# Dilated attention in one 16-stage kernel: scores in a token order by residue modulo four, run beside the last projection's matmuls

## The reference

```python
qkv = (h @ wqkv).reshape(b, s, 3, ng, A_HEADS, D_HEAD)
q, k = apply_rope(qkv[:, :, 0], cos, sin), apply_rope(qkv[:, :, 1], cos, sin)
...
wts = jax.nn.softmax(jnp.stack(lses, axis=0), axis=0)
o = jnp.sum(wts[..., None] * jnp.stack(outs, axis=0).astype(jnp.float32), axis=0).astype(h.dtype)
return o.reshape(b, s, A_HEADS * D_HEAD) @ wo
```

## Time and profile before

| | |
|---|---|
| median of 3 runs | 2399.34 us (2391.01 to 2400.08) |
| the profiled execution's own time | 2394.36 us |
| its span | 2392.5 us |
| PE busy in the span | 2285.8 us (96%) |
| DVE, ACT, POOL busy | 1485.6, 1158.6, 175.0 us |
| mean granted TensorE clock | 0.979 of 2.4 GHz |
| HBM read | 392.50 MB |

### The profile page before, as it was taken

One profiled execution on the slowest core, in us unless ns is written; L12 is line 12 of the kernel. 1 busy time (PEld: TensorE's weight loads), 2 busy tenths in 40 slices (PEclk: granted clock), 3 DMA queues, 4 the chain that ended last, 5 costly groups with the idle time before them and its releaser, 6 DMA issues.

```text
span 2392.5 us, 32798 instructions
## 1 busy us (share of the span) xinstructions
PE 2285.8 (96%) x12883; PEld 1846.9 (77%) x12883; DVE 1485.6 (62%) x2089; ACT 1158.6 (48%) x1672; POOL 175.0 (7%) x288
## 2 busy tenths in 40 slices
PE   8999899999998999799999999998999999979998
PEld 6888788887887668678877888857888788748886
DVE  6656657657665866576566657565655765647655
ACT  5445445446544453254455445444445544545444
POOL 1001001001001011310010000001000100041001
PEclk9999999999999999799999999999999999989999
DMA  7556546554656420165545555504555565506553
GB/s 246 189 182 217 184 156 210 191 190 145 213 175 214 163 99 4 37 196 179 193 167 187 192 188 195 178 18 135 178 193 184 169 193 184 194 4 207 177 184 106
DMA packets 289751, 395.68 MB, mean 165 GB/s; under 512 B 11672, under 2 KB 193248, under 8 KB 289600
## 3 DMA queue, kind: packets, MB, share of 16 engines
q1 hardware_dynamic: 284800, 377.33, 47.8%
q0 software_dynamic: 4656, 16.20, 2.0%
q10 hardware_dynamic: 144, 0.07, 0.0%
HBM read 392.50 MB, written 1.05 MB: 164 GB/s over the span
## 4 chain that ended last, share of the span: by engine, by line
PE 76%; DVE 5%; ACT 3%; issue 2%; POOL 1%; DMA 1%; DVEq 0%; POOLq 0%; ACTq 0%; SPq 0%
PE bank L490 22%; PE bank L492 22%; PE bank L491 22%; PE bank L516 1%; PE bank L1349 1%; PE bank L504 1%; ACT wh L605 1%; DVE wl L790 1%; ACT JUNK L612 1%; DVE TMP L828 1%; DVE H L848 0%; PE bank L1351 0%; PE bank L1376 0%; PE bank L1363 0%; DVE qPS L1706 0%
## 5 line engine op out<-in xcount | busy, mean ns | idle before, releaser
L790 DVE TENSOR_TENSOR wl<-raw,wh 128x1024 fp32r<-128x1024 f32 x708 | 860.5, 1225 | 586.9 <-ACT wh L605 585.8
L605 ACT ACTIVATE wh<-raw 128x1024 fp32r<-128x1024 f32 x708 | 744.1, 1058 | 673.1 <-PE bank L492 646.5
L490 PE MATMUL bank<-wh,XH 128*128 128x512 f32 x2000 | 805.2, 403 | 21.2 <-DVE XL L807 6.1
L491 PE MATMUL bank<-wl,XH 128*128 128x512 f32 x2000 | 786.1, 393 | 0.0
L492 PE MATMUL bank<-wh,XL 128*128 128x512 f32 x2000 | 785.8, 393 | 0.0
L490 PEld LDWEIGHTS bank<-wh,XH 128*128 128x128 f32 x2000 | 380.0, 190 | 110.2 <-issue 13.5
L492 PEld LDWEIGHTS bank<-wh,XL 128*128 128x128 f32 x2000 | 379.5, 190 | 82.5
L491 PEld LDWEIGHTS bank<-wl,XH 128*128 128x128 f32 x2000 | 380.4, 190 | 74.2 <-issue 0.5
L490 PE MATMUL bank<-wh,AH 128*128 128x512 f32 x704 | 276.0, 392 | 0.0
L492 PE MATMUL bank<-wh,AL 128*128 128x512 f32 x704 | 274.1, 389 | 0.0
L491 PE MATMUL bank<-wl,AH 128*128 128x512 f32 x704 | 274.1, 389 | 0.0
(11 more groups left out here) (317 smaller groups left out, 1779.0 us busy)
## 6 DMA issues: line engine op xcount, KB each, us to landing
raw<-in_ffn_w_dram SPq DMA_DIRECT2D x184, 512.0 KB, 4.7
raw<-in_ffn_wi_dram SPq DMA_DIRECT2D x176, 512.0 KB, 4.7
raw<-in_ffn_w_dram SPq DMA_DIRECT2D x40, 1024.0 KB, 4.9
raw<-in_ffn_wo_dram SPq DMA_DIRECT2D x40, 1024.0 KB, 5.0
raw<-in_a_wqkv_dram SPq DMA_DIRECT2D x18, 1024.0 KB, 4.8
raw<-in_a_w_in_dram SPq DMA_DIRECT2D x16, 1024.0 KB, 6.4
raw<-in_b_w_in_dram SPq DMA_DIRECT2D x12, 1024.0 KB, 4.9
bc<-in_norm_g_dram POOLq DMA_DIRECT2D x16, 512.0 KB, 5.2
```

Of the source, the lines that this page charges most:

```text
L490: pe.e.matmul(o, a, h, start=(k == 0), stop=False)
L491: pe.e.matmul(o, a, l, start=False, stop=False)
L605: act.e.activation(self.wh[j % N_W][:, 0:p.size], self.raw[p.chunk % N_RAW][:, p.at:p.at + p.size], ACT.Copy).then_inc(*self.rounded.up(j))
L790: dve.e.tensor_tensor(self.wl[j % N_W][:, 0:p.size], self.raw[p.chunk % N_RAW][:, p.at:p.at + p.size], self.wh[j % N_W][:, 0:p.size].bitca ...
```

## The change

Tokens are kept in the order of `order = j % 32 * 4 + j // 32` inside each tile of 128, so the 64 tokens of a half tile hold two residues modulo 4. In groups 1 and 2 a query's half tile then needs only the same half of each key tile: 128 keys, not 256. A row has 256 + 128 + 128 = 512 scores, one bank. The token order is made when the stage's input is scaled (`dve_x_scale` writes `CT` permuted), the norm's factors are permuted by a small matmul with `dCP`, and undone when the sum is split into `XH` and `XL` (`dil_out`). The masks are 512 wide and are added by DVE with the scale and the maximum in one `tensor_tensor_reduce`, not by PE. The items run beside blocks 6 to 8: item i's scores ahead of part 27 + i, its transposes two steps into the next part. The key transposes of block 5 come at step 104, not 108. The sums run once for a whole token tile, behind `in`. `out` runs tile by tile (`head=0, tail=4`).

```diff
-            add(n, "out", 4, cut(rows(A["a_wo_2"][0]), range(2)), head=2, tail=2)
+            add(n, "out", 4, cut(rows(A["a_wo_2"][0]), range(2)), head=0, tail=4)
@@ pe_turn_own, act_own, dve_own
-        if n and step == 1 and STAGES[n - 1][0] == "dilated":
-            self.pe_turn_x(pe, n, 0, 0)
-            self.pe_turn_x(pe, n, 0, 1)
...
+            if own:
+                self.act_norm(act, n, 0)
             for b in range(2):
                 self.act_x_hi(act, n, 1, b)
-            self.act_norm(act, n, 0)
-        if i == 2:
+            self.act_norm(act, n, int(own))
+        if i == 2 and not own:
             self.act_norm(act, n, 1)
@@ pe_dilated
+            part, at = divmod(step - 1, 4)
+            if step == 18:
+                self.pe_dil_rs(pe, n)
             if step == 32:
                 turn(0)
-            elif step >= 44 and (step - 44) % 16 == 0 and (step - 44) // 16 + 1 < 6:
+            elif step in (44, 60, 76, 92):
                 turn((step - 44) // 16 + 1)
+            elif step == 104:
+                turn(5)
+            elif step == 128:
+                self.n_pairs = first + 9
+            i = part - self.DIL_FIRST
+            if at == 0 and 0 <= i < 8:
+                self.pe_dil_score(pe, i, (first + 2) % 3)
+            if at == 2 and 1 <= i <= 8:
+                self.pe_dil_turn(pe, i - 1)
...
-        for i in range(10):
-            if i < 8:
-                self.pe_dil_score(pe, i, 0)
-                self.pe_dil_score(pe, i, 1)
...
+        for t in range(T):
+            self.pe_dil_sum(pe, t, (first + 1 + t) % 3)
@@ pe_dil_score
+        for u in range(2):
+            hs = self.HALF[u]
+            pe.e.matmul(banks[u][:, 0:S], self.dQT[hs, pr, t * P:(t + 1) * P], self.dKT[hs, pr, :], start=True, stop=True)
+        for g in range(1, 3):
+            for e, u in self.UNITS:
+                hs, toks = self.HALF[u], slice(t * P + e * HD, t * P + e * HD + HD)
+                keys = self.dKT[hs, 4 * g + pr, :].rearrange("p (k s) -> p k s", k=T)[:, :, self.HALF[e]]
+                m = pe.e.matmul(banks[u][self.HALF[e], (g + 1) * P:(g + 2) * P].rearrange("p (k s) -> p k s", k=T),
+                                self.dQT[hs, 4 * g + pr, toks], keys, start=True, stop=True)
@@ pe_dil_turn
+        for diagonal in range(2):
+            for c in range(S, 512, HD):
+                for u in range(2):
+                    h = self.HALF[u ^ diagonal]
+                    m = pe.e.matmul(banks[u][h, c:c + HD], x[h, u, c:c + HD], self.ident[h, h], start=True, stop=True)
+            if diagonal == 0:
+                for u in range(2):
+                    for c in range(0, S, P):
+                        pe.e.transpose(banks[u][:, c:c + P], x[:, u, c:c + P], self.ident[:, :])
@@ pe_dil_sum, pe_dil_sum_part
+            for k in range(T):
+                for e in range(2):
+                    for u in range(2):
+                        hd = slice((2 * pr + u) * HD, (2 * pr + u + 1) * HD)
+                        pe.e.matmul(banks[e][self.HALF[u], cols], self.dVD[:, k, 0, hd],
+                                    pt[:, u, k * P + e * HD:k * P + (e + 1) * HD], start=(pr == 0 and k == 0), stop=False,
+                                    skip_group_check=True)
+            self.pe_dil_sum_part(pe, banks, pt, pr, 1, False)
         pe.wait_ge(self.moved, "qkv", 8, 1)
+        for pr in range(4):
+            m = self.pe_dil_sum_part(pe, banks, self.dPT[4 * t + pr], pr, 2, pr == 3)
...
+        for k in range(T):
+            for e, u in self.UNITS:
+                h, hd = self.HALF[e], slice((2 * pr + u) * HD, (2 * pr + u + 1) * HD)
+                at = (g + 1) * P + k * HD
+                m = pe.e.matmul(banks[e][self.HALF[u], pr * HD:(pr + 1) * HD], self.dVD[h, k, g, hd], pt[h, u, at:at + HD],
+                                start=False, stop=last and k == T - 1, skip_group_check=True)
@@ act_dilated, per part k from 27
+            if k > first:
+                self.round(act, layer.parts[k - 1].j + N_W)
+                if k % 4 == 0 and k < last:
+                    take(k // 4 - 1)
+            i = k - first
+            if i < 8:
+                self.act_dil_exp(act, i)
+            if 1 <= i <= 8:
+                for u in range(2):
+                    act.wait_ge(self.turned, "dpt", i - 1)
+                    act.e.activation(self.dPT[i - 1][:, u, :], self.bank(self.place["turn", ("dpt", i - 1, u)]),
+                                     ACT.Copy).then_inc(*self.moved.up("dpt", i - 1, u))
@@ dve_dilated, per part k from 27
+            if k - first < 8:
+                self.dve_dil_top(dve, k - first)
+            if k > first:
+                self.leave(dve, layer.parts[k - 1].j + N_W)
+            if k - first < 8:
+                self.dve_dil_share(dve, k - first)
@@ dve_dil_top
+        for u in range(2):
+            dve.e.tensor_tensor_reduce(self.dPS[i % 2][:, u, :], self.banks[self.place["dscore", i]][:, u * 512:(u + 1) * 512],
+                                       self.dMK[:, i // 4, :], 0.125, -1e30, ALU.add, ALU.max,
+                                       accum_out=mx[:, u:u + 1]).then_inc(*self.made.up("dmasked", i, u))
@@ dve_dil_out
+        for b in range(2):
+            self.dve_weigh(dve, n, b, 0, self.pair((n, "out", b))[0])
+        self.dve_resid(dve, n, 0)
+        for p in parts[0:2]:
+            self.leave(dve, p.j + N_W)
+        self.dve_weigh(dve, n, 0, 1, self.pair((n, "out", 0))[1])
+        if self.goes_on(n):
+            self.dve_x(dve, n + 1, 0)
+        self.dve_weigh(dve, n, 1, 1, self.pair((n, "out", 1))[1])
+        self.dve_resid(dve, n, 1)
```

More of the change, by code:

```diff
@@ L58, in constants @@
     rope = rope.reshape(T, P, 2, 8).transpose(1, 2, 0, 3)
+    roped = rope[order]
     a = np.arange(P)
@@ L816, in dve_own @@
         if n and i == 0:
-            if STAGES[n - 1][0] == "dilated":
-                self.dve_x(dve, n, 0)
             self.dve_x(dve, n, 1)
@@ L988, in pool_out, with half @@
         f2 = (pre * factor) ** 2
-        for t in range(T):
+        def half(t):
             pool.wait_ge(self.squared, "out", n, 0, t)
@@ new lines, in pe_dilated, with pe_dil_rs @@
+        for t in range(T):
+            self.pe_dil_sum(pe, t, (first + 1 + t) % 3)
+        self.n_pairs = first + 9
+        self.linear(pe, n, "out", self.XH, self.XL, lambda k, t: [(self.moved, "o", t, 1), (self.made, "o", t, 1)],
+                    lambda b, t: [(self.weighed, n, 1, t)], lambda step: self.pe_turn_next(pe, n, "out", step))
+    def pe_dil_rs(self, pe, n):
+        rs = self.cols(T, "rs", n)
+        bank = self.turn_bank(pe, "rsp", (self.moved, "rsp"))
+        pe.wait_ge(self.rs, n, T - 1)
+        pe.wait_ge(self.moved, "dcp")
+        pe.e.matmul(bank[:, 0:T], self.dCP[:, :], rs, start=True,
+                    stop=True).then_inc(*self.product.up("rsp"))
@@ L1340, in pe_dil_score @@
+    def pe_dil_score(self, pe, i, pair):
         pr, t = i % 4, i // 4
-        hs = slice(u * HD, (u + 1) * HD)
-        for b in range(2):
-            self.take_bank(pe, 2 * u + b, (self.moved, "pr", i, u), (self.made, "max", i, u))
+        self.place["dscore", i] = pair
+        banks = [self.take_bank(pe, 2 * pair + u, (self.made, "dmasked", i, u)) for u in range(2)]
         pe.wait_ge(self.made, "qk", 5, 2)
[L1345 to L1351, removed]
@@ L1381, in act_dilated, with take @@
         layer = self.layers[n, "in"]
-        rs = self.cols(T, "rs", n)
-        for i, p in enumerate(layer.parts):
-            self.act_own(act, n, i)
+        rs = self.cols(T, "rsp", n)
+        def take(b):
+            for t in range(T):
+                to = self.dVD[:, t, b - 6, :] if b >= 6 else self.TMP[:, t, b % 2, 0:512]
+                act.wait_ge(self.used[t], layer.end[b])
+                act.wait_ge(self.moved, "rsp")
+                if b < 2:
+                    act.wait_ge(self.resid, n - 1, 1, 1)
+                elif b < 6:
+                    act.wait_ge(self.turned, "qk", b - 2, 2)
+                act.e.activation(to, self.pair((n, "in", b))[t], ACT.Copy, scale=rs[:, t:t + 1]).then_inc(
+                    *self.moved.up("qkv", b, t))
@@ new lines, in act_dilated @@
+        first, last = self.DIL_FIRST, len(layer.parts)
+        for i, p in enumerate(layer.parts[:first]):
+            self.act_own(act, n, i)
+            if i == 1:
+                act.e.activation(self.dCP[:, :].rearrange("p (c b) -> p c b", c=4), self.ident[:, :].rearrange(
+                    "p (b c) -> p c b", c=4), ACT.Copy).then_inc(*self.moved.up("dcp"))
+            if i == 3:
+                act.wait_ge(self.product, "rsp")
+                act.e.activation(rs, self.bank(self.place["turn", "rsp"])[:, 0:T], ACT.Copy).then_inc(
+                    *self.moved.up("rsp"))
```

228 lines of the change are left out of this document (117 added, 111 removed).

## The result

| | before | after |
|---|---|---|
| median (one more run of before than in the table ahead of the prediction) | 2396.69 us (4 runs, 2391.01 to 2400.08) | 2361.68 us (4 runs, 2360.4 to 2365.03) |
| the profiled execution's own time, span | 2394.36, 2392.5 us | 2365.03, 2363.2 us |

The ratio is 0.9858, with a 95% interval of 0.9834 to 0.9883: 34 us less. The forecast was 2363.0 (2350 to 2378). Two more sets of runs of the same kernel gave 0.9854 (0.9829 to 0.9878) and 0.9863 (0.9845 to 0.988).

The account below looks back on a forecast made before the run. PE, busy 96% of the span, was taken as the bound. Attention with the norm-factor matmul (-29.0) and the hand-over (-4.8) gave -33.8 us, so 2396.9 - 33.8 = 2363 us, range 2350 to 2378.

Parts of the forecast that it names:

- Attention on PE: Scores, transposes and sums of the changed stage: 35.8 us on PE in place of 65.1, 29.3 less.
- scores: Each attention item's score products on PE: 1.3 us an item, bounds 0.9 and 1.5, with the masks leaving PE.
- transposes: Each attention item's 16 quarter products with the identity and four full transposes: 2.0 us, bounds 1.4 and 2.2.
- sums: Attention's sums per token tile: 4.7 us a tile, 9.4 for both, 12.6 as the upper bound.
- The change of form: Switching PE's array between tile shapes in attention: 0.1 to 0.2 us each, 10.2 us in the sum.
- The first rival: Attention on PE: changes of form cost 0.2 or more, 128-row sums 0.11 a pair; 2371 us, chance 0.22.
- The rule of the Trainium skill: Against the change: no array mode change is free; 76 at 0.2 make 15.2 in place of 10.2, giving 2368 us.
- The interleaved stretch: Items beside value blocks: a part takes PE 6.0 us; cover 7.4 against a chain of 5.0, so no wait.
- Small products side by side: Quarter-array products in attention run four at a time, 0.11 us for four passes of 128 columns.
- Step 104 and `pe_dil_rs`: Block 5's transposes four steps earlier just fit, 0 to 0.3 us; the norm factors' matmul adds about 0.3, no wait.
- Hand-over: `out` to the next stage's first 14 matmuls: 20.4 us in place of 25.16, 4.8 less, bounds -7.5 and -3.
- Slower rival: PE waits at every item's transposes and the clock falls: 8 x 5.8 = 46 us, 2409, chance 0.03.

Follow-up runs that it names:

- e6_forms: Changed kernel with each item's four full transposes spread one by one among its quarter products, 10 changes of array form an item, not 4: 2370.68 us, ratio 0.9901.
- v_sum: Changed kernel with a tile's sums ordered by group, not alternating groups 0 and 1 by pair of heads: 2363.88 us, ratio 0.9877.
- e5_cover: Changed kernel with each item's transposes issued at the next part's first step, ahead of the next scores, not at its third: 2377.66 us, ratio 0.9912.
- e4_triple: Changed kernel with the quarter products of groups 1 and 2 of each item's scores issued three times: 2371.29 us, ratio 0.9904.
- e1_tail: Changed kernel with the output projection and hand-over to the next stage put back as before the change: 2368.40 us, ratio 0.9872.
- v_all: v_best with the sums also ordered by group as in v_sum: 2364.10 us, ratio 0.987.
- v_best: Changed kernel with DVE making the next stage's input right behind tile 0's residual, and tile 1's transposes at steps 8 and 9: 2360.39 us, ratio 0.9854.

## Why the prediction was right

The forecast of 2363 was 1.3 us from the median. The sum forecast 33.8 us less; the medians differ by 35.0, the stage by 32.6 to 34.1. That it came so near is in part luck: attention with `pe_dil_rs` saved 26.9 in place of 29.0, and the hand-over made up for it with 5.8 (7.2 where the clock stayed at 2.4 GHz) in place of 4.8. Medians of one kernel alone differ by 6 us between the three sets. The terms:

- **Attention on PE**: forecast 35.8 in place of 65.1, -29.3. Measured: B less 55.19, A 26.68 more, the first scores ahead of A 1.3 more, together -27.2. The direction and the mechanism hold. Three terms were somewhat small: scores 1.44 not 1.3, transposes 2.02 not 2.0, sums 4.96 a tile not 4.7. The change of form, measured at 0.15 (e6_forms, v_sum), explains most of what the sums lack, and nothing else: there it was taken at 0.1 for ten changes a tile, and the timeline shows eight, as groups 1 and 2 follow each other in one form. In the scores and transposes the sum already had it at 0.14 and 0.15. Why the scores take 0.14 more, over half of the 2 us, no experiment separates. The first rival's other half, the 128-row sums at 0.11 a pair, fell: 0.063 at most.
- **The rule of the Trainium skill**, "TensorEngine Tiling (Array Packing)", Key Properties, that changing the tiling mode drains TensorE: the trace agrees that no change is free. The prediction counted 76 changes; the timeline of after has 73, seven for each item and 17 in the sums. At 0.146 they are 10.7 us; the sum had 10.2 and the upper bound from rows 4 15.2.
- **The interleaved stretch**: no wait forecast, none found. The chain is 4.2 us, not 5.0, since its instructions overlap the readouts behind them, against a cover that I put at 7.4. e5_cover, with the cover cut to the four steps, waits 1.45 us, and this is the 4.2 less 2.7.
- **Small products side by side**: as forecast (e4_triple: 0.109 for four).
- **Step 104 and `pe_dil_rs`**: no wait; the small product adds 0.28 us.
- **Hand-over**: forecast 20.4, measured 19.3 where the clock falls and 17.7 where it doesn't. The wait was 2.34, not 3.1: two `leave` took 2.26 of DVE's queue, and CT, XH, XL overlapped more than in rows 9. Of the forecast 0.5 for tile 1's residual about 0.2 appeared, and only where the clock stayed at 2.4 GHz (D is 14.31 there, else 14.07 to 14.09 with this hand-over). The cost of the clock, 1.7, was 1.6. That the order of the lists brings the gain, and not the sums ahead of it, is what e1_tail shows.
- **Slower rival** (2409): its place and its wait appear when the cover is taken away, but waits of 1.45 us left the clock at 2.4 GHz. Waits of over 2 us at every item, which it asked for, were in no run.

What stays open: why one profile of after kept the clock, what makes the two pauses in the sums, and what the time in the stages outside the change differs by from run to run (the stretch before the stage); no run looked at that.

## What to carry to other kernels

Price small products by their slots from start to start, per concurrent group, and count each change of the array's form as a term of its own. Whether a chain of other engines is hidden is one subtraction, cover less chain. Put into a list that the next stage waits for first what it waits for, but look again at what then stands last: all three versions that gained in C lost some of it in D.

## What the runs showed of the hardware that I had not expected

- A change between array forms costs 0.146 us on average of full to quarter and back (48 changes, 6.99 us), and 0.15 between 128x64 and quarters (six changes, 0.92 us).
- Passes in quarters start every 0.016 us at most: 128 in 2.02 us, the change of form behind them included (v_sum). An fp32 product is two passes, so a product takes 0.03 us. The Trainium skill, "TensorE: Matmul & The Clock Gate", "Wait — 56ns, not 53.3ns?", gives about 25 ns as the least from the start of one matmul to that of the next. Counted by passes, which are the records here, four tiles side by side went below it, and for them the measurement decides; counted by products they did not.
- A run of 384 such short passes paused twice for 0.42 to 0.45 us with no releaser, both times at the same two passes (v_sum, v_all). With more changes of form between them the same passes took 10.25 us of B in place of 9.9 and did not pause in the first profile of after, but e4_triple and v_best lost 0.3 to 0.4 us at one of these two places each. What makes the pause no run shows.
- The same wait of 2.34 us on the same instruction left the clock at 2.4 GHz in one profile and was followed by about 3.4 us at 1.2 GHz in eight.
